# Weight loads requested by GpSimd instead of SyncE in a 528-unit float32 matmul stream

## The reference

```python
# layer A/B: h = rms_norm(x); p = h @ ab_w_in; gated linear attention and
#            forgetting attention on slices of p, gated; x += mix @ ab_w_out
# layer C:   h = rms_norm(x); u, gate = h @ c_w_in; a state-space scan (S5),
#            a gated linear unit (glu_w); x += mix @ c_w_out; then the final norm
# two layers of the second block:
def second_block(x, norm_w, w_in, ..., w_out):
    for l in range(2):
        h = rmsnorm(x, norm_w[l])
        proj = jnp.einsum("bsd,de->bse", h, w_in[l])
        y_ssd = ssd_branch(...)            # Mamba-2, chunked
        y_cfm = conformer_branch(...)      # depthwise convolution
        y_att = diff_attention_branch(...) # differential attention
        x = x + jnp.einsum("bse,ed->bsd", concat(y_ssd, y_cfm, y_att), w_out[l])
```

## Time and profile before

| | |
|---|---|
| median of 3 runs | 3325.62 us (3324.76 to 3325.98) |
| the profiled execution's own time | 3327.72 us |
| its span | 3325.9 us |
| mean granted clock of TensorE | 0.997 |
| PE busy | 3290.1 us, 99% |
| DVE, ACT, POOL busy | 2080.6, 1263.9, 146.9 us |
| 16 DMA engines | one hardware queue, 578.16 MB, 51.8% busy |
| loads of weights | 528 of 512 KB, median 3.6 us from request to landing |

### The profile page before, as it was taken

How to read it: one execution, slowest core, us unless ns; L and a number is a source line. 1 busy time by engine, 2 the same in 40 slices (tenths; PEclk the granted TensorE clock), 3 DMA queues, 4 the chain that set the end, 5 groups by cost and what they waited for, 6 DMA issues and landing times.

```text
span 3325.9 us, 42719 instructions
## 1 busy us (share of the span) xinstructions
PE 3290.1 (99%) x15690; PEld 2677.0 (80%) x15690; DVE 2080.6 (63%) x3161; ACT 1263.9 (38%) x1987; POOL 146.9 (4%) x116
## 2 busy tenths in 40 slices
PE   8999999999999999999999999999999999999999
PEld 7888887787888888888888887787778888778777
DVE  5665656687765655534264786667756477666763
ACT  4333324445443344523142225424534223532541
POOL 3000000001020000000020000100002000000000
PEclk9999999999999999999999999999999999999999
DMA  5333435677776665746452443444547354345445
GB/s 177 128 121 105 138 127 186 222 243 267 254 261 207 192 204 179 244 171 209 151 186 99 156 159 130 153 134 165 200 160 252 107 173 148 131 142 169 169 164 203
DMA packets 297712, 580.88 MB, mean 175 GB/s; under 512 B 63768, under 2 KB 110616, under 8 KB 297504
## 3 DMA queue, kind: packets, MB, share of 16 engines
q1 hardware_dynamic: 297504, 578.16, 51.8%
HBM read 445.90 MB, written 132.14 MB: 174 GB/s over the span
## 4 chain that ended last, share of the span: by engine, by line
PE 82%; issue 12%; DVE 3%; DMA 1%; ACT 1%; POOLq 1%; DVEq 1%; SPq 0%; ACTq 0%
PE bank L560 62%; PE bank L559 10%; PE bank L2015 1%; PE bank L1596 1%; PE bank L1100 1%; POOLq L462 1%; PE bank L737 1%; PE bank L1421 1%; PE bank L1130 1%; PE bank L1452 1%; PE bank L1608 1%; DMA convert_in<-x 0%; PE bank L1610 0%; PE bank L1006 0%; DVE weights_low L472 0%
## 5 line engine op out<-in xcount | busy, mean ns | idle before, releaser
L560 PE MATMUL bank<-act_high,weights_high 128*128 128x512 f32 x3584 | 1426.6, 398 | 13.6 <-DVE act_low L543 11.3
L560 PE MATMUL bank<-act_low,weights_high 128*128 128x512 f32 x3584 | 1403.4, 392 | 0.0
L472 DVE TENSOR_TENSOR weights_low<-weights_raw,weights_high 128x1024 fp32r<-128x1024 f32 x528 | 654.4, 1240 | 752.3 <-ACT weights_high L403 740.7
L403 ACT ACTIVATE weights_high<-weights_raw 128x1024 fp32r<-128x1024 f32 x528 | 558.5, 1058 | 1443.8 <-PE bank L560 1200.5
L560 PE MATMUL bank<-act_high,weights_low 128*128 128x512 f32 x3584 | 963.3, 390 | 0.0
L560 PEld LDWEIGHTS bank<-act_high,weights_high 128*128 128x128 f32 x3584 | 676.4, 189 | 164.7 <-DVE act_low L543 11.3
L560 PEld LDWEIGHTS bank<-act_low,weights_high 128*128 128x128 f32 x3584 | 677.2, 189 | 135.7 <-issue 1.2
L560 PEld LDWEIGHTS bank<-act_high,weights_low 128*128 128x128 f32 x3584 | 673.1, 188 | 139.6
L559 PE MATMUL bank<-weights_high,act_high 128*128 128x512 f32 x640 | 253.9, 397 | 3.9 <-DVE stream_out L501 3.1
L559 PE MATMUL bank<-weights_high,act_low 128*128 128x512 f32 x640 | 249.8, 390 | 0.0
L2113 DVE SCALAR_TENSOR_TENSOR residual_in<-residual_in,arena 128x512 f32<-128x512 f32 x240 | 182.1, 759 | 20.9 <-issue 2.4
(11 more groups left out here) (325 smaller groups left out, 2576.5 us busy)
## 6 DMA issues: line engine op xcount, KB each, us to landing
weights_raw<-in_w_all SPq DMA_DIRECT2D x528, 512.0 KB, 3.6
convert_in<-mix SPq DMA_DIRECT2D x80, 256.0 KB, 4.5
fm_b<-stream_out SPq DMA_DIRECT2D x72, 256.0 KB, 2.6
mix<-arena SPq DMA_DIRECT2D x64, 256.0 KB, 3.2
x_part<-stream_out SPq DMA_DIRECT2D x48, 256.0 KB, 4.5
residual_in<-x_part SPq DMA_DIRECT2D x48, 256.0 KB, 5.5
x<-stream_out SPq DMA_DIRECT2D x48, 256.0 KB, 5.4
convert_in<-x SPq DMA_DIRECT2D x48, 256.0 KB, 4.2
```

The costliest lines, as they stand in the source:

```text
L403: e.activation(WH[:, t % 3, :], RAW[:, t % 3, :], ACT.Copy).then_inc(wh_ready, 1)
L472: e.tensor_tensor(WL[:, t % 3, :], RAW[:, t % 3, :], WH[:, t % 3, :].bitcast(F32), ALU.subtract).then_inc(wl_ready, 1)
L560: return e.matmul(bank[s][:, :], a[:, s * P:(s + 1) * P], h, start=start, stop=stop)
```

## The change

The function `weights_sp` becomes `weights_pool`, with the same wait and the same transfer, and GpSimd calls it. GpSimd requests units 0, 1 and 2 first, and then, at the head of each slot t from 0 on, unit t+3, ahead of its squares and masks of that slot. SP requests everything else in the order it had. Buffers, semaphores and all other engines are as before.

```diff
-        def weights_sp(e, t):
+        def weights_pool(e, t):
             if t >= 3:
                 e.wait_ge(wl_ready, t - 2)
             e.dma_start(RAW[:, t % 3, :], I["w_all"][PASSES[UNITS[t][0]].group, UNITS[t][1]]).then_inc(raw_in[t % 3], 16)
@@ @block.sync
             e.dma_start(GAIN[:, 0:5, :], I["gains"]).then_inc(gain_in, 16)
-            weights_sp(e, 0)
             for n in BY_SLOT[-1]:
                 convert_sp(e, n)
-            weights_sp(e, 1)
-            weights_sp(e, 2)
...
             for n in BY_SLOT[0]:
                 convert_sp(e, n)
-            weights_sp(e, 3)
-            weights_sp(e, 4)
...
                 take(t)
-                if t + 5 < NU:
-                    weights_sp(e, t + 5)
@@ @block.gpsimd
+            for t in range(3):
+                weights_pool(e, t)
             take, finish = stages(e, "pool")
             for t in range(-1, NU):
+                if t >= 0 and t + 3 < NU:
+                    weights_pool(e, t + 3)
                 for n in BY_SLOT.get(t, ()):
                     convert_pool(e, n)
                 take(t)
```

## The result

The change makes the kernel slower: 3353.43 us (median of 4 runs, 3352.07 to 3355.31) against 3325.80 (4 runs, 3324.76 to 3326.45), a ratio of 1.0078 with the interval 1.0065 to 1.0091, or +27.6 us. The forecast was 3324.2, the range ended at 3340: the time lies outside it, on the side of the rival called "POOL's loads are slow to land". The profiled execution took 3352.07 us with a span of 3350.2, 24.3 more than before (the medians differ by 3.3 us more, since the profiled execution of the kernel before was slower than its median and that of the changed kernel faster); the mean granted clock is 0.995 against 0.997.

The account below looks back on a forecast made before the run. PE was taken to bound the kernel. Start +0.2, statistics +1.8, 0, 0 and +0.3, forgetting attention -3.0 and S5 -0.7 sum to -1.4 us, taking 3325.62 to 3324.2; range 3317 to 3340.

Parts of the forecast that it names:

- POOL's loads are slow to land: Rival, slower: from landings of about 5.6 us the loop through POOL's adds sets the pace; 3342.5 us at 7; chance 0.22.
- What bounds the kernel: Whole kernel: PE is busy 3290.1 of 3325.9 us, so only some 36 us can be won back.
- The landing time: Weight loads on POOL: 4.4 us from request to landing, 0.8 of it for POOL's part; bounds 3.0 and 9.0.
- What is queued behind what on POOL: Slots with squares or masks: POOL's next load waits behind its adds, which matters at the four statistics.
- first statistic: Load goes out after the last add at 46.70, so PE waits +1.8 us; bounds +0.4 and +6.4.
- second: Second statistic: load lands 1.8 us late, but PE's transpose has 2.6 us of room; cost 0.
- fourth: Fourth statistic: PE's wait of 0.8 us goes, a late load adds 1.1; net +0.3 us, bounds -0.8 and about +7.
- DVE and POOL at once: Low parts slowed 1.1 us beside POOL's work are taken as hidden by whole units of room: 0; upper bound +4.
- Third statistic: Its last add is 4.7 us before ACT's need, more room than at the second; cost 0.
- The start: PE's first matmul: unit 0, requested by POOL at about 0.75, lands at 5.15; +0.2 us, bounds -1.2 and +4.8.
- Forgetting attention: SP no longer stands on a weight load: 2.0 us of PE's wait, 1.0 of low clock; -3.0, bounds -4.6 and +1.0.
- S5: S5 scan: without the weight load in SP's burst, PE's 2.3 us wait shrinks by 0.7; bounds -3.9 and 0.

Follow-up runs that it names:

- experiment 1: Changed kernel, the drain after each of POOL's adds of squares replaced by a semaphore wait on the add before: 3337.17 us, 1.0029.
- experiment 2: Kernel before the change, with the same replacement of the drain by a semaphore wait in POOL's adds: 3325.78 us, 1.0000.
- experiment 7: Kernel of experiment 1, with POOL's adds over 8 of the 512 columns, other columns' sums left out: 3333.00 us, 1.0015.
- Experiment 6: Kernel of experiment 1, with the load of unit 0 alone requested by SP again: 3340.32 us, 1.0036.
- Experiment 4: Kernel before the change, with SP's one weight load ahead of forgetting attention's first loads moved behind them: 3323.36 us, 0.9985.
- experiment 5: Kernel of experiment 1, with the loads of units 374 and 502 held until an activation tile PE needs next has landed: 3335.05 us, 1.0020.
- experiment 9: Changed kernel with the edits of experiment 1, experiment 5, Experiment 6 and experiment 7 together, other columns' sums left out: 3326.72 us, 0.9998.

## Why the prediction was wrong, step by step

**What bounds the kernel**: right. PE stayed the engine that sets the time, and all of the loss is PE's idle time and low clock.

**The landing time**: right within 0.6 us. 4.4 forecast, 3.8 measured; the 0.8 us allowed for POOL's part was too much (the request costs 0.2 us more than SP's).

By the Trainium skill's rule on the shared port ("SBUF — State Buffer", section "SBUF: two separate sides"), which is about certain DVE operations only, a transfer would be an estimated 2.5 us late (from its 620 ns that became some 3100). The trace does not show it: 322 of the 528 requests ran while DVE was busy for over 300 ns of them, and their loads landed after 3.8 us at the median, the others after 4.2. Nor does the trace show the 6 us for loading code that the Trainium skill names ("GPSIMD Engine Reference", section "Instruction dispatch"): POOL's first request starts at 1.26 us, and its load has landed at 6.4.

**"What is queued behind what on POOL": the step that failed.** It had the right places and the right sign: the load of unit s+3 goes out behind the last add. But it took the time of that last add from the kernel before, as if POOL's own order stayed as fast. It never names the drain: the 0.16 us of "issue" ahead of each second add in the earlier trace rows went into its sums unseen and unchanged, and no term stood for its growing. That was the price of a drain with no transfer of its own engine to wait for. With one just requested it is up to 5.9 us, ahead of the add on which the next request depends. The terms came out as: first statistic +5.6 instead of +1.8, second +2.9 instead of 0 (of which the 1.1 at unit 144 is not the drain's, as experiment 1 keeps it), fourth +6.0 instead of +0.3. Experiment 1 gives it its size, 16.3 us; experiment 2 shows that it needs both parts.

**The rival "slow to land"** had 0.22 and the loop (load, high part, squares, add, next load), and put the time at 3342.5. Its condition, landings over 5.6 us, was met by 105 of the 528 loads, but not by the typical one (3.8 us). Its loop closed by another way: by the drain the landing counted twice, once for ACT and once for the adds. The range stopped at 3340 since only that condition was priced; nothing stood in it for an instruction of POOL's whose meaning changes with what POOL has requested.

**"DVE and POOL at once: 0"**: wrong by 1.6 us in this kernel. The hindrance of 1.1 us was read rightly in the earlier trace rows, and taken as hidden since low parts have whole units of room. The room is not the low part's, it is that of the eviction behind it on DVE. Third statistic +1.6 (in e1 +4.2); experiment 7 shows the cause, and 4.2 us in the medians. That the 528 requests themselves would not hinder DVE was right: with the adds narrowed, the 6 low parts that ran beside a request took 1.22 to 1.23 us.

**The start: +0.2 forecast, +1.6 measured.** The landing of unit 0 was priced like any other, 4.4 us, from a request at 0.75. The request starts at 1.26, and the load takes 5.2 us. In the changed kernel POOL requests three loads at once, x3 from 1.26 us, beside SP's first activations:

```profile
1.26 1.72 POOL L323 DMA_DIRECT2D weights_raw<-in_w_all  x3 [0.81 <-POOLq L2863]
...
6.51 1.28 ACT L403 ACT_TABLE_LOAD   x1 [6.51 <-DMA weights_raw<-in_w_all]
...
12.96 0.80 PE L560 MATMUL bank<-act_high,weights_high 128*128 128x512 f32 x1 [12.96 <-DVE act_low L543]
```

It landed at 6.4 and not 5.15. The bounds (-1.2 to +4.8) held it. Experiment 6 shows that what is crowded only changes: the first load or the first activations.

**Forgetting attention: -3.0 forecast, -3.8 net measured** (-4.88 at unit 81, of which 2.95 is the wait; +1.08 behind it). Right in place and mechanism, and partly lucky in size: some 1.7 us of the 4.88 is the spell of low clock, and the kernel of experiment 2, which has the same wait, has no spell behind it. SP reads on as soon as the store has landed, 1.5 us after the request (526.65 to 528.19 in the changed kernel), where I took 3.0:

```profile
526.65 0.35 SPq L1333 DMA_DIRECT2D fox_rows<-arena  x1
528.19 1.77 SPq L1385 DMA_DIRECT2D arena<-fox_rows  x4
```

Experiment 4 shows that this gain is had alone, without moving the other 527 loads.

**S5: -0.7 forecast, +2.2 measured, outside the bounds (-3.9 and 0).** SP does finish its burst earlier: from its first L394 store to the end of the eight L1556 requests 12.4 us instead of 13.2. But PE starts later, 19.4 us behind that store instead of 17.3, as these rows of the changed kernel show, SP first, then PE:

```profile
1276.60 2.53 SPq L394 DMA_DIRECT2D fm_c<-stream_out  x4
...
1285.12 3.84 SPq L1556 DMA_DIRECT2D arena<-s_u  x8
...
1296.04 3.64 PE L1596 MATMUL bank<-arena 128*128 128x64 f32 x16 [4.49 <-issue]
```

My reading is that the transfers lose time to the weights' queue, whose loads of 1281.21 and 1287.10 are not behind them any more. This is the second failing thought: I priced SP's queue only as a cost, and not as the order in which urgent and patient transfers reach the engines. No term stood for it; if the S5 scan is counted in, it is 9.5 us of the steps at 371, 372, 499 and 195. At 371 and 499 experiment 5 shows it. In the S5 scan it is argued from the trace, not tried: PE's longest wait at L1596 is 2.7 to 4.5 us in the other six traces with the weights on a queue of their own and 2.1 to 2.3 in the four with all on SP's, but in that of experiment 7, which has two queues as well, it is 2.3.

**The sum.** With the four causes taken away and the gain in forgetting attention kept, the time is that of the kernel before within the spread (experiment 9: 0.9998). The drain's share is shown by itself, 16 to 18 us. Those of the other three are not, since one by one their edits gave less than together. Which of the smaller steps is queue and which is clock stays open: half-clock spells lie elsewhere from trace to trace even between kernels that hardly differ (experiment 2 has PE's stalls of the earlier trace rows without the spells behind them).

## What to carry to other kernels

Before DMA requests are moved to another engine, read that engine's drains: one that cost 0.16 us may from then on wait for each transfer just requested. A queue that many transfers share is also their order of urgency; loads that have 11 us of margin, put on a queue of their own, take bandwidth from tiles that have none. And where only one stall in 528 loads is worth removing, move that one load: 4.0 us gained, against 27.6 lost.

## What the runs showed of the hardware

- A drain on POOL behind a DMA request of POOL lasted until that transfer had landed: all 23 drains that found such a load under way ended 72 to 83 ns behind its landing, with POOL idle up to 5.9 us; of 55 that found a load of SP under way, 54 did not wait for it. With a semaphore between the adds in its place the kernel is 16.3 us faster.
- A request of a 512 KB load takes 527 ns of POOL, 333 of SP, 334 of ACT; it lands after 3.8, 3.6 and 3.5 us at the median.
- Two-input operations of DVE and POOL at the same time slow each other: low parts of 2.3 us instead of 1.2. A DMA request of POOL beside a low part did not: with the adds narrowed, the 6 low parts beside a request took 1.22 to 1.23 us, and the slowest of all 528, beside a narrow add, 1.44.
